# In the first attention, TensorE takes the values product of one task ahead of the transposes of the next

## The reference

```
diff  (6 heads): p = softmax(q.k*scale - slope*dist) for two maps m; a = p0 - lam*p1; o = a @ v
chunk (4 heads): o = softmax(q.k*scale + bias) @ v
mla   (6 heads): o = softmax((qn.kn + qr.kr)*scale) @ v
x = x + concat(norm(o_mla), norm(o_diff), norm(o_chunk)) @ w_out
x = x + conv_ffn(norm(x))
```

## Time and profile before

| | |
|---|---|
| median of 3 runs | 3231.89 us (3230.84 to 3237.18) |
| the profiled execution's own time | 3240.42 us |
| its span | 3238.7 us |
| TensorE matmul busy | 3112.6 us, 96% of the span |
| VectorE, ScalarE, GpSimd busy | 41%, 25%, 42% |
| share of the chain that ended last | PE 91%, DVE 4%, issue 2%, ACT 1%, DMA 1% |
| lines 513 to 515 in that chain | 25%, 24%, 24% |
| lines 691, 714, 704 in that chain | 3%, 2%, 1% |
| mean granted TensorE clock | 0.964 of full speed |

### The profile page before, as it was taken

One profiled execution on the slowest core, in us unless ns is written; L12 is line 12 of the kernel. 1 busy time (PEld: TensorE's weight loads), 2 busy tenths in 40 slices (PEclk: granted clock), 3 DMA queues, 4 the chain that ended last, 5 costly groups with the idle time before them and its releaser, 6 DMA issues.

```text
span 3238.7 us, 40314 instructions
## 1 busy us (share of the span) xinstructions
PE 3112.6 (96%) x13950; PEld 2448.0 (76%) x13950; DVE 1324.1 (41%) x2953; ACT 809.4 (25%) x1811; POOL 1363.7 (42%) x924
## 2 busy tenths in 40 slices
PE   7989999999899999999999999999999999999998
PEld 6767788888667788878666778888686667788886
DVE  5476434244574534353630741112337307411113
ACT  3345212122244212121333221101213333210112
POOL 4211555564211555554222445555352234455552
PEclk9888999999879999999999999999999999999999
DMA  6211566664222566655233556566452235456663
GB/s 239 91 53 53 183 194 194 192 214 153 91 65 79 180 194 187 201 177 176 84 97 112 158 167 193 189 189 202 130 182 91 89 113 157 155 189 189 206 192 102
DMA packets 136518, 494.06 MB, mean 153 GB/s; under 512 B 15280, under 2 KB 15536, under 8 KB 136112
## 3 DMA queue, kind: packets, MB, share of 16 engines
q0 software_dynamic: 66240, 241.20, 24.2%
q1 hardware_dynamic: 68544, 245.40, 23.3%
q10 hardware_dynamic: 1584, 5.40, 0.5%
HBM read 489.84 MB, written 2.10 MB: 152 GB/s over the span
## 4 chain that ended last, share of the span: by engine, by line
PE 91%; DVE 4%; issue 2%; ACT 1%; DMA 1%; POOL 0%; DVEq 0%; SPq 0%; POOLq 0%; ACTq 0%
PE ps L513 25%; PE ps L514 24%; PE ps L515 24%; PE ps L744 3%; PE ps L769 3%; PE ps L691 3%; PE ps L714 2%; PE ps L640 1%; PE ps L641 1%; PE ps L642 1%; PE ps L704 1%; PE ps L757 1%; PE ps L902 1%; DVE small L1086 1%; PE ps L921 0%
## 5 line engine op out<-in xcount | busy, mean ns | idle before, releaser
L513 PE MATMUL ps<-hi,w_hi 128*128 128x512 f32 x3216 | 1294.1, 402 | 34.2 <-POOL w_lo L486 15.2
L514 PE MATMUL ps<-hi,w_lo 128*128 128x512 f32 x3216 | 1268.1, 394 | 0.0
L515 PE MATMUL ps<-lo,w_hi 128*128 128x512 f32 x3216 | 1266.7, 394 | 0.0
L486 POOL TENSOR_TENSOR w_lo<-w_raw,w_hi 128x1024 fp32r<-128x1024 f32 x460 | 1105.8, 2404 | 104.8 <-DMA w_hi<-weights 95.3
L481 POOL DMA_DIRECT2D w_hi<-weights x460 | 261.4, 568 | 1728.2 <-PE ps L515 1573.6
L513 PEld LDWEIGHTS ps<-hi,w_hi 128*128 128x128 f32 x3216 | 612.5, 190 | 233.6 <-issue 94.9
L515 PEld LDWEIGHTS ps<-lo,w_hi 128*128 128x128 f32 x3216 | 612.9, 191 | 131.7
L514 PEld LDWEIGHTS ps<-hi,w_lo 128*128 128x128 f32 x3216 | 613.8, 191 | 121.0
L1120 DVE CUSTOM_DVE_ANT_0 pr<-ps,kc 128x128 f32<-128x128 f32 (+2 forms) x160 | 65.3, 408 | 340.8 <-PE ps L744 340.8
L1803 ACT ACTIVATE ps<-hb,col 128x512 f32<-128x512 f32 x88 | 68.5, 782 | 381.1 <-DVE hb L1062 381.1
L1538 DVE SCALAR_TENSOR_TENSOR x<-x,ps 128x512 f32<-128x512 f32 x64 | 43.9, 687 | 287.1 <-PE ps L515 287.1
(11 more groups left out here) (317 smaller groups left out, 3235.5 us busy)
## 6 DMA issues: line engine op xcount, KB each, us to landing
w_raw<-weights SPq DMA_DIRECT2D x460, 512.0 KB, 3.8
w_hi<-weights POOLq DMA_DIRECT2D x460, 512.0 KB, 4.5
x<-xt SPq DMA_DIRECT2D x8, 256.0 KB, 10.4
out<-x SPq DMA_DIRECT2D x8, 256.0 KB, 2.1
kc<-k ACTq DMA_DIRECT2D x1, 1281.0 KB, 5.8
bias<-relb ACTq DMA_DIRECT2D x2, 512.0 KB, 5.4
bias<-relb ACTq DMA_DIRECT2D x1, 1024.0 KB, 5.0
praw<-pt ACTq DMA_DIRECT2D x2, 512.0 KB, 3.6
```

The source lines that it names most:

```text
L486: nc.gpsimd.tensor_tensor(wlo[s][:, :], raw[s][:, :], whi[s][:, :].bitcast(F32), ALU.subtract).then_inc(w_split, 1)
L513: nc.tensor.matmul(out_ap, w[0], xx[0], start=first, stop=False)
L514: nc.tensor.matmul(out_ap, w[1], xx[0], start=False, stop=False)
L515: return nc.tensor.matmul(out_ap, w[0], xx[1], start=False, stop=last)
```

## The change

The block for the values product of task it-3 stands ahead of the block for the transposes of task it-2. Nothing else is moved; both blocks keep their waits. In an iteration TensorE now makes the scores of task it+1, the fill, the values product of task it-3, and the transposes of task it-2.

```
                     if it >= 0:
                         fill(it)
+                    if 0 <= it - 3 < n:
+                        i, t = it - 3, ts[it - 3]
+                        pe.wait_ge(pt_ready, t.id + 1)
+                        if t.more.get("value"):
+                            pe.wait_ge(d_free[BANK[t.more["value"]]], USE[t.more["value"]] + 1)
+                        for kb, v in enumerate(t.vs):
+                            last = nc.tensor.matmul(ps[:, TO_BANK[i % 3], 0:64], slots(i)[1][t.id % 2][:, kb * P:(kb + 1) * P], v,
+                                                    start=(kb == 0), stop=(kb == len(t.vs) - 1))
+                        last.then_inc(pv_done, 1)
                     if 0 <= it - 2 < n:
                         i, t = it - 2, ts[it - 2]
                         ... (waits for p_ready or exp_done, and for on_ready; then the transposes, t_done)
                         q.task += 1
-                    if 0 <= it - 3 < n:
-                        ... (the same block as above)
                 q.on += n
```

## The result

The changed kernel takes 3260.07 us, the median of 6 runs (3254.06 to 3268.81), against 3232.44 (3220.64 to 3238.55, 6 runs) for the kernel before on the same chip: ratio 1.0084, 95% interval 1.0064 to 1.0104, which is 27 us slower (21 to 34). The forecast was 3249, 17 us slower, with a range of 3231 to 3261, of which the result keeps within 1 us of the upper end, and a narrower own range of 3241 to 3258, which it misses by 2 us.

What follows compares the result with a forecast made beforehand. TensorE was taken to bound the kernel, 91% of the chain that ended last. Terms of 8.4 us in the first layer and 8.2 in the second gave 17 us, so 3231.9 becomes 3249, range 3231 to 3261.

Steps and rivals of the forecast that it cites:

- Term 1, no fill: From iteration 37 on, values products wait for their own copy: 0.6 us per round, 2.2 and 2.0 us.
- upper bound: Without fill, 0.8 us per round if each stalled product also shows the load of its stationary block.
- Term 2, the end: At the end of the list, the last products wait for their copies, delaying the output projection: 1.9 us per layer.
- Term 3: In diff tasks with fill, the score reader starts later and the second score map waits for it: 4.6 us per layer.
- first two kinds: Second map held up by the reader: 0.55 us each at four tasks, 0.7 us once, per layer.
- third kind: At tasks 27 and 31 the reader leads a gapless VectorE chain; all of V4, 0.84 us, is lost, twice.
- low bound of 0: Lowest size for the diff tasks with fill: 0 us, if there is cover that was not seen.
- The gain: Scaling starts earlier since the product no longer waits behind transposes; at one fill wait, -0.4 us per layer.
- The faster rival (3222): VectorE's earlier start at the scaling, not the score reader, decides: 3220 to 3226 us; chance 0.1.
- the same 17 us: Step from the profiled execution, 3240.4 to 3257 us, to the median, 3231.9 to 3249 us, as waits of fixed length.
- rival of the clock: New waits cause one more half-clock stretch per layer, +12 us on the sum: 3260 us; chance 0.13.
- Absorbed (3236): VectorE has unseen cover in diff tasks; only low ends without fill and at the list's end remain, 4 us; chance 0.2.

Runs made afterwards that it cites:

- e4: The changed kernel with eight score slots in place of six from task 25 on; 3243.82 us.
- e9: Kernel before, with the new order only in iterations 6, 22, 23, 26, 27, 30 and 31; ratio 1.0005, +2 us.
- e10: Kernel before, with the new order in iterations before 37 except 6, 22, 23, 26, 27, 30 and 31; ratio 1.0021, +7 us.
- e2: Kernel before, with the new order only up to iteration 36, under the fill; 3249.94 us.
- e3: Kernel before, with the transposes moved ahead of the fill, right behind the scores, product left behind the fill; 3193.72 us.
- e11: Kernel before, with transposes ahead of the fill only in iterations 0 to 7 and 18 to 31; 3199.57 us.
- e5: Kernel before, with product, then transposes, then fill behind the scores up to iteration 36; 3191.53 us.
- e12: Kernel before, with the fill moved behind both blocks: scores, transposes, product, fill in every iteration; 3184.8 us.
- e7: Kernel before, with transposes right behind the scores, ahead of the fill, and eight score slots from task 25 on; 3204.02 us.

## Why the prediction was right, and where its sizes were off

The direction and two of the three mechanisms hold as written; of the third, the size holds and the path is wrong in part. The size was 17 and is 27 us, of which 18 to 22 are left at equal clock. The wide range holds by 1 us and the own range, 3241 to 3258, does not; with all runs at the upper clock of the changed kernel (0.967, 3254 to 3256 us) it would have held: on which side of it the median falls is the luck of the clock.

- **Term 1, no fill, 2.2 + 2.0 us.** Right in kind, small in size. The stalls are 0.25 and 0.14 us (0.26 and 0.15 computed), but a round grew by 0.81 us, not by the 0.6 that I took. What I had named as the upper bound, the exposed load of the stationary block, is there: every product holds TensorE some 0.10 us longer. By the starts of the scores the stretch from task 43 on costs 2.9 us in the first layer and 2.9 in the second, the chunk tasks included.
- **Term 2, the end, 1.9 per layer.** It measures 3.05. My sum began at the product of two blocks. From there it is 2.53, since three products wait for their copies and not two; the other 0.5 lies before that point, where I had taken the start as the same in both orders.
- **Term 3, 4.6 per layer.** The steps have about the size that was worked out: 0.62 for 0.55, 0.84 for 0.7, 0.85 for 0.84. The second map waits for the reader as written in the first two kinds. For the third kind, the two steps of 0.84 ("there all of V4, 0.84, is lost, twice"), the path was wrong in part: I had it start at the reader alone, and in e4, where the reader is free, both steps stay, because ScalarE's copy and the emptying of a projection bank behind it hang on the same transposes. That V4 was lost in full there was right for a reason that I had not seen. The low bound of 0 is refuted in the traces of e9 and e10, place by place, and in time by e2. e3 and e11 show from the other side that what the transposes release is on the path.
- **The gain, -0.4 per layer.** The scaling did start earlier (74.0 us of waits became 62.2), and nothing came of it that the runs can tell. The faster rival (3222) is refuted: the scaling started earlier, the reader later, and the kernel became slower.
- **The clock.** The step that failed is the one that carried "the same 17 us" from one execution to the median, since "the terms are waits of fixed length". The runs of the changed kernel have a lower mean clock than those of before (0.964 on average against 0.968), and this is 5 to 9 us. So the rival of the clock holds in part, in about the size that I gave it for one layer (6 us), though the profiled execution, with the higher clock, cannot show where; and not at its place: the stretch without fill in the first layer, with its many short waits, ran at full clock (changed kernel, columns as in the earlier trace rows):

```profile
258.00:301.00 43.00, 40.44 (x240) 27.62 (x240) 28.55 (x158) 27.95 (x81) 7.57 (x5) 1.00 0.23 74
```

  TensorE stood idle 2.56 us of 43 in short waits, and the clock stayed up. By the rule of the Trainium skill on frequent short idle times (TensorE: Matmul & The Clock Gate, A second HAM failure mode: psum-queue depth-cycling) it would go down here; this trace does not agree.

- **Absorbed (3236).** Refuted by the interval, 21 to 34 us.

## What to carry to other kernels

In an ordered queue ask of each block what it releases, and how far behind the previous release it stands; the order of two neighbours matters less than what stands between them and the work that waits for them. Here swapping them cost 27 us, and moving both ahead of the fill won 46. A product whose stationary operand is what another engine has just written loses the hidden weight load as well as the wait; count both. And where the clock differs from kernel to kernel, a sum of waits gives only the part at equal clock: compare runs at equal mean clock before judging a term. Ask also for every queue behind a block, not only for the longest one: here freeing VectorE's reader left TensorE waiting for ScalarE at the same place.

## What had not been expected of the hardware

- The granted clock makes a third to two thirds of the gain of the fast versions (e3, e5, e11, e12). The kernel before alone took 3227 us at a mean clock of 0.970 (mean of 9 runs) and 3243 at 0.962 (mean of 2); over all its runs it is 2.5 us for each 0.001. In e3 and e12, with idle time in the stages of 25.7 and 24.1 us where it was 39.3, the clock rose to 0.90 to 0.92; in the changed kernel, with 48.1 us idle, it was 0.88 in the profiled run against 0.86 before. So less idle time went with a higher clock in e3, e5, e11 and e12, but this is no rule: e7 had only 24.6 us idle (228.6 - 214.2 and 222.1 - 211.9) and a clock of 0.87 and 0.89.
- A kernel with fewer waits need not be the faster one: e7 is 10 us above e3, although at equal clock it is 1 to 3 us below.
